# Four modulation blocks of layer 0 moved behind the first feed-forward units, and layer 1's column sums taken two units later, in a two-block fp32 kernel

## The chip, the cores and the metric

The kernel runs on one core of one Trainium2 chip. The metric is the device time of one execution in microseconds (us); the median of the runs shown is quoted. The tensor engine (TensorE, PE in the profile) multiplies, the vector engine (VectorE, DVE) and the scalar engine (ScalarE, ACT) evacuate and prepare operands, GpSimd (POOL) helps, and SyncE (SP) issues nearly all weight transfers from one in-order queue.

## The reference, cut to what matters

The program computes two blocks on a latent sequence of 512 rows and a context of 256 rows, width 1024, all in fp32. Only the first block matters here. It has two layers, a Fourier mixer layer (i = 0) and a differential attention layer (i = 1), and each begins with its modulation vectors:

```
for i in range(DEPTH):
    sh1, sc1, g1, sh2, sc2, g2 = split(silu(c)     @ w_ada[i] + b_ada[i], 6)
    csh1, csc1, cg1, csh2, ...  = split(silu(c_ctx) @ w_ada[i] + b_ada[i], 6)
    x = x + g1 * mixer(modulate(rms_norm(x), sh1, sc1))
    x = x + g2 * swiglu(modulate(rms_norm(x), sh2, sc2), ffn_w_in[i], ffn_w_out[i])
    (the same for ctx, in layer 0)
```

So each layer has a matrix w_ada[i] of 1024 x 6144 (24 MB) that is multiplied with only two vectors (the latent's condition and the context's). The kernel cuts it into 24 blocks of 256 columns, 1 MB each. Blocks 0 to 3 give sh1, 4 to 7 sc1, 8 to 11 g1, 12 to 15 sh2, 16 to 19 sc2 and 20 to 23 g2. The last four of layer 0, which give g2, are used only when a product of the first feed-forward is added to x.

## The kernel before, in words

**One stream of weights.** `stream_plan` writes down every weight block in the order in which it is loaded, and SP issues the loads in that order. The first 24 loads (`EARLY`) rotate over six buffers (two of `ring` and four of `early`, which are later overwritten by the split weights); all later ones alternate over the two buffers of `ring`. Before SP issues a load it waits until the block before it in the same buffer has been used (`blocks_used`), and everything behind it in the queue waits too.

**The front.** The order is: 24 modulation blocks of layer 0, four blocks of the Fourier layer's output weights (`fnet`, each from two sources, 4 transfers), then the feed-forward. In the front TensorE runs the DFT of x, and in between takes each modulation block as strips: `ada_rows` multiplies its eight 128-row pieces with the two conditions in four 32-column strips of the array (L677), VectorE copies the result to SBUF, `ada_cols` turns and sums it into columns (L688), and VectorE adds the bias. Blocks 16 to 19 of the order come beside the last DFT feature products; then comes `dft_middle` (L785), then blocks 20 to 23 in a loop of their own, then `x_turned` (L758, L760) for four pieces of x, the meta rows (L827), and the first `fnet` product (L845). The first `fnet` block is prepared by GpSimd (a sum and a difference of its halves, L2965 and L2967), split by ScalarE (`split_hi`, which waits until all 24 front blocks have been used) and VectorE (`split_lo`).

**Split weights.** Every weight block of 128x2048 is split into a high and a low part (ScalarE L1682, VectorE L2359) into one of two buffers, two units ahead of TensorE: in the slot after unit c the block of unit c+2 is split. TensorE makes three products for each piece of 128 rows (high by high, high by low, low by high).

**The first feed-forward.** A layer's feed-forward has 22 "in" units and three groups of four "down" units: in 0 to 7, down 0 to 3 of group 0, in 8 to 15, down 0 to 3 of group 8, in 16 to 21, down 0 to 3 of group 16 (with 6 pieces instead of 8). A unit is 96 matmuls (L649 with 512 columns, L654 with 256). After an in unit ScalarE and VectorE gate it (L2464, L2467), ScalarE rounds `hid`, VectorE makes its low part (L2471), and the split follows; after a down unit VectorE adds to x (`residual`, L2445).

**Layer 1's modulation beside it.** Its 24 blocks are streamed between the units: block k comes directly behind the weights of unit k+1. Blocks 0 to 21 are summed by VectorE at the end of the slot of in unit k (`sum_ada`: 16 instructions of 128x256, L2272 and L2275), and TensorE takes the column sums at the end of in unit k+1 (`ada_reduce`, eight small matmul records, L698), waiting for VectorE's `ada_acc`. Blocks 22 and 23 are taken as strips on TensorE (`strips` L709 and `strip_cols` L716) beside the down units of the last group. There is no modulation block beside the other down units.

Of the kernel before, what the change touches and what calls it, by code (L numbers as in the profile page):

```python
# [12 lines left out]
P = 128  # L13
D = 1024
KC = D // P
# [14 lines left out]
EARLY = 24  # L30
# [58 lines left out]
ADA0 = [4, 5, 6, 7, 0, 1, 2, 3] + list(range(8, 24))  # L89
# [42 lines left out]
def stream_plan():  # L132
# [3 lines left out]
    for layer in range(2):  # L136
        late = []
        for lo, hi in GROUPS:
            units = [("in", layer, c) for c in range(lo, hi)] + [("down", layer, lo, cb) for cb in range(4)]
            for unit in units:  # L140
                plan += [unit] + late
                late = []
                if layer == 0 and unit[0] == "in":
                    late = [("ada", 1, unit[2])]
                elif (layer, hi) == (0, FC) and unit[3] < 2:
                    late = [("ada", 1, FC + unit[3])]
        if layer == 0:
            plan += DIFF
# [16 lines left out]
def bass_two_blocks_kernel(nc, io, kt_d, dl_d, dc_d, xsave, out):  # L165
# [36 lines left out]
    with ExitStack() as ctx:  # L202
# [234 lines left out]
        def blocks_used(key):  # L437

            if key[0] == "ada":
                if key[1] and key[2] < FC:  # L440
                    return ada_acc, key[2] + 1
                return ada_row, 25 + key[2] - FC if key[1] else AT0[key[2]] + 1
            if key in NARROW:
                return q_lo, 4 * Q_OF[key] + 4
            return w_lo, W_OF[key] + 1
# [174 lines left out]
        def _(pe):  # L620
# [70 lines left out]
            def ada_reduce(b):  # L691

                pe.wait_ge(ada_acc, b + 1)
                pe.wait_ge(ada_taken, 24 + b - 1)
                for j in range(2):
                    for c in range(2):
                        o = 4 * j + 2 * c
                        m = nc.tensor.matmul(bank[6 + b % 2][:, o:o + 2], adacc[:, b % 2, c, P * j:P * j + P], ones[:, 0:2],  # L698
# [3 lines left out]
            def strips(b):  # L702

                n = N_OF[("ada", 1, b)]
                pe.wait_ge(ring_ready[slot_of(n)], arrived(n))
                pe.wait_ge(ada_taken, 24 + b - 1)
                for kc in range(KC):
                    q = 32 * (kc % 4)
                    m = nc.tensor.matmul(bank[6 + b % 2][q:q + 32, 0:256], condz[:, kc, :], slot(n)[:, kc, :], start=kc < 4, stop=kc >= 4)  # L709
                m.then_inc(ada_row, 1)  # L710

            def strip_cols(b):

                pe.wait_ge(ada_ev, 24 + b - FC + 1)
                for j in range(2):
                    m = nc.tensor.matmul(bank[6 + b % 2][:, 256 + 2 * j:258 + 2 * j], adacc[:, b % 2, 0, P * j:P * j + P], sel,  # L716
                                         start=True, stop=True)
                m.then_inc(ada_done, 1)

            def norm_sums(i, with_ctx):  # L720
# [3 lines left out]
                if i == 1:  # L724
                    pe.wait_ge(ada_taken, 24)
# [93 lines left out]
            for i in range(20, 24):  # L819
                ada_rows(i)  # L820
                ada_cols(i - 1)
            ada_cols(23)
# [1403 lines left out]
        def _(dve):  # L2226
# [17 lines left out]
            def take_ada(layer, b):  # L2244

                dve.wait_ge(ada_done, 24 * layer + (b if layer else AT0[b]) + 1)
                o, o2 = 48 * layer + 2 * b, 2 if layer and b < FC else 1
                c = 256 if layer and b >= FC else 0
                src = bank[6 + b % 2][:, c:c + 4 * o2].rearrange("p (a n k) -> p a n k", a=2, k=o2)[:, :, :, 0]
# [3 lines left out]
            def ada_out(i):  # L2253
# [5 lines left out]
                if i:  # L2259
                    take_ada(0, ADA0[i - 1])  # L2260

            def sum_ada(b):

                n = N_OF[("ada", 1, b)]
                dve.wait_ge(ring_ready[slot_of(n)], arrived(n))
                dve.wait_ge(ada_done, 24 + b - 1)
# [108 lines left out]
            take_ada(0, ADA0[7])  # L2375
# [15 lines left out]
            for i in range(20, 24):  # L2391
                ada_out(i)
            take_ada(0, 23)
# [62 lines left out]
            def ffn(layer):  # L2456
                end = ROWS if layer == 0 else LAT
                for g, (lo, hi) in enumerate(GROUPS):
                    for k in range(lo, hi):
# [14 lines left out]
                        if layer == 0:  # L2474
                            if k:
                                take_ada(1, k - 1)
                            sum_ada(k)
                    for cb in range(4):
                        residual(T_OF[("down", layer, lo, cb)], layer, 5, cb, layer == 0)
                        split_lo(S_OF[("down", layer, lo, cb)] + NS)  # L2480
                        if (layer, hi) == (0, FC) and cb < 3:
                            take_ada(1, FC - 1 + cb)
                            if cb < 2:
                                dve.wait_ge(ada_row, 25 + cb)
                                nc.vector.tensor_copy(adacc[:, cb, 0, :], bank[6 + cb][:, 0:256]).then_inc(ada_ev, 1)
# [686 lines left out]
```

## Time and profile before

| | |
|---|---|
| median of 3 runs | 2629.66 us (2626.38 to 2633.78) |
| the profiled execution's own time | 2629.45 us |
| its span, first to last instruction | 2627.7 us |
| TensorE busy | 2443.8 us, 93% of the span |
| VectorE, ScalarE, GpSimd busy | 1274.8, 904.7, 379.5 us |
| mean granted TensorE clock | 0.963 |
| the front up to the first `fnet` product | 124.2 us |
| the first feed-forward, from in unit 1 to the last down unit | 193.3 to 777.4 us |

Times in the trace count from the first instruction. The busy time of TensorE says how full it is, not whether it is fast: a matmul at half clock is busy for longer. So the waits of TensorE and its granted clock are read together.

### The profile page before, as it was taken

The numbers are of one execution on the slowest core, as the hardware profiler recorded it, in microseconds if no ns is written. First come the engines' busy times: TensorE is split into PE (matmuls) and PEld (weight loads), VectorE is DVE, ScalarE is ACT, GpSimd is POOL, SyncE is SP. The second block draws the span as 40 slices with busy tenths as digits, with TensorE's granted clock in tenths as the row PEclk, the third lists the DMA queues.
The fourth block names the chain that finished last, engine by engine and source line by source line (L and its number), as shares of the span: only waits on it lengthen the run. The fifth ranks groups of instructions, "written<-read, shape, count | busy, mean of one in ns | idle before, by whom it ended". The sixth has DMA issues, their size and how long they took to land.

```text
span 2627.7 us, 34491 instructions
## 1 busy us (share of the span) xinstructions
PE 2443.8 (93%) x14270; PEld 2041.1 (78%) x14270; DVE 1274.8 (49%) x2067; ACT 904.7 (34%) x1480; POOL 379.5 (14%) x311
## 2 busy tenths in 40 slices
PE   7799999999989999979999989898989989999998
PEld 3588788888868777657888869787878768777777
DVE  1585534544546777764333354455554344444433
ACT  2241111111223544433222234454545233444421
POOL 0230000000015534310000010322334210000000
PEclk9899999999999999989999989899999989999998
DMA  9823332332431111012333331121211121111222
GB/s 319 238 81 96 106 103 81 113 112 65 121 120 33 42 39 49 33 48 80 97 96 96 88 120 49 33 65 65 65 49 65 49 65 50 55 59 49 80 96 89
DMA packets 252064, 220.71 MB, mean 84 GB/s; under 512 B 7352, under 2 KB 243283, under 8 KB 251524
## 3 DMA queue, kind: packets, MB, share of 16 engines
q1 hardware_dynamic: 248392, 217.86, 26.8%
q8 instruction: 113, 1.85, 0.3%
q10 hardware_dynamic: 3260, 0.58, 0.1%
q14 instruction: 43, 0.35, 0.0%
q0 software_dynamic: 256, 0.07, 0.0%
HBM read 214.23 MB, written 6.26 MB: 84 GB/s over the span
## 4 chain that ended last, share of the span: by engine, by line
PE 54%; ACT 5%; DVE 5%; issue 3%; POOL 2%; DMA 0%; DVEq 0%; POOLq 0%; ACTq 0%
PE two L649 10%; PE bank L1430 4%; PE bank L649 3%; PE bank L1246 3%; PE bank L1250 3%; PE bank L1230 3%; PE two L1192 3%; PE bank L1411 2%; PE bank L979 2%; PE bank L1113 2%; PE two L1450 2%; PE two L1087 1%; PE two L1207 1%; PE bank L949 1%; PE bank L961 1%
## 5 line engine op out<-in xcount | busy, mean ns | idle before, releaser
L2370 DVE TENSOR_TENSOR wL<-ring,wH 128x512 fp32r<-128x512 f32 x224 | 171.2, 778 | 264.4 <-ACT wH L1691 264.2
L2359 DVE TENSOR_TENSOR wL<-ring,wH 128x2048 fp32r<-128x2048 f32 (+1 forms) x80 | 179.0, 2237 | 229.3 <-ACT wH L1682 229.0
L1682 ACT ACTIVATE wH<-ring 128x2048 fp32r<-128x2048 f32 (+1 forms) x80 | 149.4, 1868 | 351.2 <-DMA ring<-in_ffn_w_out 75.1
L649 PE MATMUL two<-h1H,wH 128*128 128x512 f32 x496 | 197.2, 398 | 0.0
L649 PE MATMUL two<-h1L,wH 128*128 128x512 f32 x496 | 194.9, 393 | 0.0
L649 PE MATMUL two<-h1H,wL 128*128 128x512 f32 x496 | 194.8, 393 | 0.0
L1691 ACT ACTIVATE wH<-ring 128x512 fp32r<-128x512 f32 x224 | 134.0, 624 | 69.0 <-PE bank L1230 29.2
L2275 DVE SCALAR_TENSOR_TENSOR adacc<-ring,cond,adacc 128x256 f32<-128x256 f32 x308 | 123.8, 478 | 0.0
L2974 POOL TENSOR_TENSOR rstd<-rstd,sq 128x768 f32<-128x768 f32 (+1 forms) x15 | 30.7, 2044 | 612.5 <-ACT sq L1718 611.4
L1250 PE MATMUL bank<-unH,wH 128*128 128x272 f32 (+1 forms) x384 | 117.9, 307 | 0.0
L1753 ACT ACTIVATE gateS<-two 128x512 f32<-128x512 f32 x44 | 26.3, 598 | 262.6 <-PE bank L654 105.0
L1250 PE MATMUL bank<-unH,wL 128*128 128x272 f32 (+1 forms) x384 | 111.1, 289 | 0.0
L1250 PE MATMUL bank<-unL,wH 128*128 128x272 f32 (+1 forms) x384 | 111.1, 289 | 0.0
L649 PEld LDWEIGHTS two<-h1H,wL 128*128 128x128 f32 x496 | 94.2, 190 | 20.3
L649 PEld LDWEIGHTS two<-h1H,wH 128*128 128x128 f32 x496 | 94.5, 191 | 18.8
L649 PEld LDWEIGHTS two<-h1L,wH 128*128 128x128 f32 x496 | 94.5, 190 | 18.8
L2445 DVE SCALAR_TENSOR_TENSOR xT<-two,ada,xT 128x512 f32<-128x512 f32 (+1 forms) x48 | 30.6, 679 | 153.3 <-PE bank L654 51.7
L649 PE MATMUL two<-hidH,wH 128*128 128x512 f32 x264 | 104.1, 394 | 0.0
L649 PE MATMUL two<-hidL,wH 128*128 128x512 f32 x264 | 103.4, 392 | 0.0
L649 PE MATMUL two<-hidH,wL 128*128 128x512 f32 x264 | 103.2, 391 | 0.0
L2137 ACT ACTIVATE probA<-two,amx 128x144 f32<-128x144 f32 (+3 forms) x64 | 34.7, 541 | 154.7 <-DVE amx L2842 154.6
L1430 PE MATMUL bank<-unH,wH 128*128 128x512 f32 x192 | 83.6, 436 | 0.5 <-ACT vA L2110 0.5
(600 smaller groups left out, 6994.7 us busy)
## 6 DMA issues: line engine op xcount, KB each, us to landing
ring<-in_ffn_w_in SPq DMA_DIRECT2D x88, 512.0 KB
ring<-in_w_in SPq DMA_DIRECT2D x40, 1024.0 KB
ring<-in_w_ada SPq DMA_DIRECT2D x32, 1024.0 KB
early<-in_w_ada SPq DMA_DIRECT2D x16, 1024.0 KB, 11.3
ring<-in_ffn_w_out SPq DMA_DIRECT2D x16, 1024.0 KB
ring<-in_diff_w_in SPq DMA_DIRECT2D x12, 1024.0 KB
ring<-in_w_proj_ssd SPq DMA_DIRECT2D x8, 1024.0 KB
ring<-in_ffn_w_out SPq DMA_DIRECT2D x8, 768.0 KB
```

The costliest lines, as they stand in the source:

```text
L649: m = nc.tensor.matmul(bank[3 * s + half], w, r[:, 0:LAT], start=i == 0, stop=i == n - 1)
L979: m = nc.tensor.matmul(bank[b][:, 256 * (i % 2):256 * (i % 2) + 256], h2[x][:, kc, i * P:(i + 1) * P], w[y][:, kc, :], start=k == 0, stop= ...
L1192: m = nc.tensor.matmul(o[:, at:at + hi - lo], w[y][:, kc, P * j:P * j + P], a[x][:, kc, lo:hi], start=k == 0, stop=k == 3 * KC - 1)
L1230: m = nc.tensor.matmul(bank[b], w[y][:, kc, P * t:P * t + P], ys[x][:, kc, :], start=k == 0, stop=k == 11)
L1246: m = nc.tensor.matmul(bank[b][:, 256 * (t % 2):256 * (t % 2) + 256], un[x][:, kc, META + P * t:META + P * t + P], w[y][:, kc, :], start=k ...
L1250: m = nc.tensor.matmul(bank[b][:, 0:hi - lo], w[y][:, kc, P * j:P * j + P], un[x][:, kc, lo:hi], start=k == 0, stop=k == 3 * KC - 1)
L1430: m = nc.tensor.matmul(bank[6 + j], w[y][:, kc, P * j:P * j + P], un[x][:, kc, META:ALL], start=k == 0, stop=k == 3 * KC - 1)
L1682: nc.scalar.activation(hi, raw, ACT.Copy).then_inc(w_hi, 1)
L1691: nc.scalar.activation(hi[:, 2 * r:2 * r + 2, :], raw[:, 2 * r:2 * r + 2, :], ACT.Copy, scale=colA[:, c:c + 1] if SPLIT[n][0] == "ps" else ...
L2275: m = nc.vector.scalar_tensor_tensor(out=o, in0=w[:, kc, :], scalar=x, in1=o, op0=ALU.mult, op1=ALU.add)
L2359: nc.vector.tensor_tensor(lo, raw, hi.bitcast(F32), ALU.subtract).then_inc(w_lo, 1)
L2370: nc.vector.tensor_tensor(lo, raw, hi.bitcast(F32), ALU.subtract).then_inc(q_lo, 1)
```

## The change

Layer 0's last four modulation blocks (20 to 23) leave the front: `EARLY` is 20, the stream goes from the 20th modulation block directly to `fnet`, and ScalarE's first split waits for 20 blocks. A list `MORE` has the 28 blocks that are left (layer 0's four, then layer 1's 24), and `MORE_AT` gives each unit of the first feed-forward its block: every in unit and the first three down units of each group, in order, until the 28 are placed (in units 0 to 7 take blocks 0 to 7 of the list, down units 0 to 2 of group 0 take 8 to 10, in 8 to 15 take 11 to 18, down 0 to 2 of group 8 take 19 to 21, in 16 to 21 take 22 to 27). Each is streamed directly behind the weights of the next unit. The first four, layer 0's, are taken as strips by TensorE at the end of in units 0 to 3. All 24 of layer 1 are now summed by VectorE (two more than before), and TensorE takes the column sums of a block at the end of the second unit after the block's own (`sum_cols(j - 2)`), not of the first. VectorE waits for layer 0's 24th block before the first residual.

```diff
-EARLY = 24
+EARLY = 20
-ADA0 = [4, 5, 6, 7, 0, 1, 2, 3] + list(range(8, 24))
+ADA0 = [4, 5, 6, 7, 0, 1, 2, 3] + list(range(8, EARLY))
+MORE = [("ada", 0, b) for b in range(EARLY, 24)] + [("ada", 1, b) for b in range(24)]
+NSTRIP = 24 - EARLY
+MORE_AT = {key: j for j, key in enumerate(sum([[("in", 0, c) for c in range(lo, hi)] + [("down", 0, lo, cb) for cb in range(3)]
+                                              for lo, hi in GROUPS], []))}
...
             for unit in units:
                 plan += [unit] + late
-                late = []
-                if layer == 0 and unit[0] == "in":
-                    late = [("ada", 1, unit[2])]
-                elif (layer, hi) == (0, FC) and unit[3] < 2:
-                    late = [("ada", 1, FC + unit[3])]
+                j = MORE_AT.get(unit, len(MORE))
+                late = MORE[j:j + 1]
...
+            def more_columns(key):
+
+                j = MORE_AT.get(key)
+                if j is None:
+                    return
+                if 1 <= j <= NSTRIP:
+                    strip_cols(j - 1)
+                if j < NSTRIP:
+                    strips(j)
+                if NSTRIP <= j - 2 < len(MORE):
+                    sum_cols(j - 2)
...
             dft_middle()
-            for i in range(20, 24):
-                ada_rows(i)
-                ada_cols(i - 1)
-            ada_cols(23)
+            ada_cols(EARLY - 1)
...
-                        if layer == 0:
-                            ada_reduce(c - 1)
+                        more_columns(("in", layer, c))
...
-                        if (layer, hi) == (0, FC):
-                            if cb == 0:
-                                ada_reduce(FC - 1)
-                            if cb in (1, 2):
-                                strip_cols(FC + cb - 1)
-                            if cb < 2:
-                                strips(FC + cb)
+                        more_columns(("down", layer, lo, cb))
...
+            def more_sums(key):
+
+                j = MORE_AT.get(key)
+                if j is None:
+                    return
+                if j < NSTRIP:
+                    strip_out(j)
+                if 1 <= j <= NSTRIP:
+                    take_ada(EARLY + j - 1)
+                if NSTRIP <= j - 2 < len(MORE):
+                    take_ada(EARLY + j - 2)
+                if NSTRIP <= j < len(MORE):
+                    sum_ada(j)
...
-            for i in range(20, 24):
-                ada_out(i)
-            take_ada(0, 23)
+            take_ada(EARLY - 1)
...
                         split_lo(S_OF[("in", layer, k)] + NS)
-                        if layer == 0:
-                            if k:
-                                take_ada(1, k - 1)
-                            sum_ada(k)
+                        more_sums(("in", layer, k))
                     for cb in range(4):
+                        if (layer, g, cb) == (0, 0, 0):
+                            dve.wait_ge(ada_taken, 24)
                         residual(T_OF[("down", layer, lo, cb)], layer, 5, cb, layer == 0)
                         split_lo(S_OF[("down", layer, lo, cb)] + NS)
-                        if (layer, hi) == (0, FC) and cb < 3:
-                            take_ada(1, FC - 1 + cb)
...
+                        more_sums(("down", layer, lo, cb))
```

`sum_cols` and `ada_reduce` issue the same matmuls; `strips` and `strip_cols` are the functions of before with another index.

## Rows read from the trace of the kernel before

**Rows 1.** The page's line of engines: busy us, share of the span, instructions.
```profile
PE 2443.8 (93%) x14270; PEld 2041.1 (78%) x14270; DVE 1274.8 (49%) x2067; ACT 904.7 (34%) x1480; POOL 379.5 (14%) x311
```
**Rows 2.** TensorE's waits from 96 to 173 us: total, times, longest.
```profile
PE bank L677 <- DMA early<-in_w_ada: 4.3, 2, 4.2
```
**Rows 3.** TensorE's waits from 193.3 to 777.4 us, the first feed-forward.
```profile
PE bank L698 <- DVE adacc L2275: 12.0, 7, 3.1
PE bank L709 <- DMA ring<-in_w_ada: 3.4, 1, 3.4
```
**Rows 4.** Windows: length, TensorE busy (matmuls), granted clock, DMA share, GB/s.
```profile
104.00:124.00 20.00, 10.18 (x56) 0.51 0.41 93
...
285.00:292.00 7.00, 6.14 (x19) 0.51 0.75 226
...
482.00:490.00 8.00, 7.25 (x22) 0.57 0.85 240
...
728.00:739.00 11.00, 6.55 (x31) 0.54 0.65 205
```
**Rows 5.** Timeline of SyncE, 92 to 108 us: start, duration, what.
```profile
95.18 2.86 SPq L573 DMA_DIRECT2D ring<-in_fnet_w_out  x1
```
**Rows 6.** Timeline of all engines, 108 to 125 us; idle before in brackets.
```profile
112.06 2.82 POOL L2965 TENSOR_TENSOR wsum<-ring 128x1024 f32<-128x1024 f32 x1 [15.67 <-DMA ring<-wback]
...
112.53 2.38 DVE L2403 TENSOR_SCALAR ng<-ada 128x16 f32<-128x16 f32 x1
...
118.31 1.03 PE L827 MATMUL bank<-kt,mraw 16*128 16x16 f32 x8
...
124.06 0.60 SPq L573 DMA_DIRECT2D ring<-in_fnet_w_out  x1
...
124.18 0.66 PE L845 MATMUL two<-uvH,wH 128*128 128x386 f32 x1 [4.83 <-DVE wL L2357]
```
**Rows 7.** Windows of 1 us (length, granted clock, DMA share, GB/s) behind that issue.
```profile
131.00:132.00 1.00, 1.00 0.15 46
```
**Rows 8.** Timeline of TensorE at 96, 210, 228 and 750 us.
```profile
96.36 1.51 PE L785 MATMUL two<-RS,kt 128*32 128x257 f32 x32
...
209.96 0.95 PE L698 MATMUL bank<-kt,adacc 128*128 128x2 f32 x8
...
227.56 0.95 PE L698 MATMUL bank<-kt,adacc 128*128 128x2 f32 x8
...
750.16 0.50 PE L716 MATMUL bank<-kt,adacc 128*128 128x2 f32 x4
...
751.59 0.50 PE L649 MATMUL two<-hidH,wH 128*128 128x512 f32 x1
```
**Rows 9.** Timeline of VectorE, 193 to 213 us: the slot of in unit 0.
```profile
194.48 0.69 DVE L2464 TENSOR_TENSOR gateS<-gateS,two 128x512 f32<-128x512 f32 x1 [4.95 <-ACT gateS L1756]
...
196.41 0.96 DVE L2471 TENSOR_TENSOR hidL<-gateS,hidH 128x768 fp32r<-128x768 f32 x1 [0.91 <-ACT hidH L1760]
198.22 2.29 DVE L2359 TENSOR_TENSOR wL<-ring,wH 128x2048 fp32r<-128x2048 f32 x1 [0.85 <-ACT wH L1682]
...
200.95 5.63 DVE L2275 SCALAR_TENSOR_TENSOR adacc<-ring,cond,adacc 128x256 f32<-128x256 f32 x14
211.14 0.69 DVE L2464 TENSOR_TENSOR gateS<-gateS,bank 128x512 f32<-128x512 f32 x1 [4.56 <-ACT gateS L1756]
```
**Rows 10.** Timeline of SyncE, 420 to 545 us: loads of modulation blocks.
```profile
422.97 0.37 SPq L591 DMA_DIRECT2D ring<-in_w_ada  x1
...
521.13 0.37 SPq L591 DMA_DIRECT2D ring<-in_w_ada  x1
...
539.83 0.37 SPq L591 DMA_DIRECT2D ring<-in_w_ada  x1
```
**Rows 11.** Timeline of VectorE, 376 to 396 us: two down units without blocks.
```profile
376.44 2.19 DVE L2445 SCALAR_TENSOR_TENSOR xT<-two,ada,xT 128x512 f32<-128x512 f32 x4 [12.29 <-PE two L654]
...
393.12 0.75 DVE L2445 SCALAR_TENSOR_TENSOR xT<-two,ada,xT 128x512 f32<-128x512 f32 x1 [12.29 <-PE bank L654]
```

More of the change, by code:

```diff
@@ L437, in blocks_used @@
         def blocks_used(key):
+            if key in MORE:
+                j = MORE.index(key)
+                return (ada_row, EARLY + j + 1) if j < NSTRIP else (ada_acc, j - NSTRIP + 1)
             if key[0] == "ada":
-                if key[1] and key[2] < FC:
-                    return ada_acc, key[2] + 1
-                return ada_row, 25 + key[2] - FC if key[1] else AT0[key[2]] + 1
+                return ada_row, AT0[key[2]] + 1
             if key in NARROW:
@@ L689, in ada_cols, with strips @@
                 m.then_inc(ada_done, 1)
[L691 to L695, printed above, removed]
+            def strips(j):
+                n = N_OF[MORE[j]]
+                pe.wait_ge(ring_ready[slot_of(n)], arrived(n))
+                pe.wait_ge(ada_taken, EARLY + j - 1)
+                for kc in range(KC):
+                    q = 32 * (kc % 4)
+                    m = nc.tensor.matmul(bank[6 + j % 2][q:q + 32, 0:256], condz[:, kc, :], slot(n)[:, kc, :], start=kc < 4, stop=kc >= 4)
+                m.then_inc(ada_row, 1)
@@ new lines, in strip_cols, with sum_cols @@
+            def strip_cols(j):
+                pe.wait_ge(ada_ev, EARLY + j + 1)
+                for h in range(2):
+                    m = nc.tensor.matmul(bank[6 + j % 2][:, 256 + 2 * h:258 + 2 * h], adacc[:, j % 2, 0, P * h:P * h + P], sel,
+                                         start=True, stop=True)
+                m.then_inc(ada_done, 1)
+            def sum_cols(j):
+                pe.wait_ge(ada_acc, j - NSTRIP + 1)
+                pe.wait_ge(ada_taken, EARLY + j - 1)
+                for h in range(2):
@@ L696, in ada_reduce @@
                     for c in range(2):
-                        o = 4 * j + 2 * c
-                        m = nc.tensor.matmul(bank[6 + b % 2][:, o:o + 2], adacc[:, b % 2, c, P * j:P * j + P], ones[:, 0:2],
+                        o = 4 * h + 2 * c
+                        m = nc.tensor.matmul(bank[6 + j % 2][:, o:o + 2], adacc[:, j % 2, c, P * h:P * h + P], ones[:, 0:2],
                                              start=True, stop=True)
                 m.then_inc(ada_done, 1)
[L702 to L718, printed above, removed]
+            def more_columns(key):
[8 more added lines that the diff above has]
+                    sum_cols(j - 2)
@@ L724, in norm_sums @@
                 if i == 1:
-                    pe.wait_ge(ada_taken, 24)
+                    pe.wait_ge(ada_taken, EARLY)
                 for k, x in enumerate((part, sq[:, 0], sq[:, 1])):
@@ L2242, in _, with take_ada @@
             nc.vector.tensor_copy(negR[:], negm).then_inc(s_round, 1)
[L2244 to L2249, printed above, removed]
+            def take_ada(i):
+                dve.wait_ge(ada_done, i + 1)
+                _, layer, b = (("ada", 0, ADA0[i]) if i < EARLY else MORE[i - EARLY])
+                o, k, c = 48 * layer + 2 * b, 2 if i >= 24 else 1, 256 if EARLY <= i < 24 else 0
+                src = bank[6 + i % 2][:, c:c + 4 * k].rearrange("p (a n k) -> p a n k", a=2, k=k)[:, :, :, 0]
                 nc.vector.tensor_tensor(ada[layer][:, 2 * b:2 * b + 2, :], src,
@@ L2374, in _ @@
                 ada_out(i)
-            take_ada(0, ADA0[7])
+            take_ada(7)
             multipliers(0)
```

14 lines of the change are left out of this document (8 added, 6 removed).

## The prediction, made before the changed kernel was run

> **What bounds the kernel now.** I read the page first. TensorE is busy 93% of the span [rows 1], so its waits are few and each is worth finding; the other engines have room on average. Then I listed TensorE's waits in the two stretches that the change touches. In the front it waits 4.3 us for the modulation blocks, almost all of it for block 23, and 4.8 us for the first `fnet` weights [rows 2, 6]. In the first feed-forward it waits 12.0 us in seven places for VectorE's sums and 3.4 us for one strip block [rows 3]. Third, the windows with the granted clock: it is at the lower of its two levels (0.5, 1.2 GHz) from about 104 to 128 us after TensorE had idled, and again after three of the waits in the feed-forward [rows 4]. Last, the timelines of SyncE, VectorE and TensorE, to see who is late for whom.
>
> **The front.** Removed: four loads of 1 MB, four times strips and columns on TensorE, four copies and additions on VectorE. Today `dft_middle` starts at 96.36 [rows 8] and ends at 97.9; the four blocks and the wait for the last fill the time to 110.3, then come `x_turned` and the meta rows, which end at 118.31 + 1.03 = 119.34, and the first `fnet` product starts 4.84 us later, behind ScalarE's and VectorE's split [rows 6]. After the change the chain is: ada_cols of block 19 to about 98.3; `x_turned` 4 at 99.3 (it needs the last feature copy); its third piece needs VectorE, which after 99.3 has some 2 us of small work and one copy, so about 102.3; meta rows done at 105.7 (the same instructions with the clock still up for most of them); plus 4.84: 110.6. The other chain into the same start is the load. Its first issue is at 95.18 [rows 5], behind strips 18 and not behind the four blocks, so it hardly moves; today its data come through a queue that still holds 4 MB and GpSimd starts on them at 112.06 [rows 6], while the third `fnet` block, alone in the queue, is issued at 124.06 [rows 6] and its traffic ends in the microsecond after 131 [rows 7], some 7.4 us later. So the first lands near 102.5, GpSimd needs 2.8 + 2.4 us, ScalarE and VectorE 2.3 us behind that, and this chain ends near 110. The two meet; I take 110.6, a gain of 124.2 - 110.6 = 13.6 us. What follows (four `fnet` blocks, norm, modulation) hangs on this start and moves with it. Bounds: 9 us if the `fnet` load is no faster than today relative to its neighbours, 15.5 if the clock stays up.
>
> There is a collision in this stretch. VectorE's `ng`, sixteen columns, took 2.38 us and ended when GpSimd's sum that began 0.47 us earlier ended [rows 6]. The Trainium skill, SBUF — State Buffer, Who interferes with whom, says that the two share a port pair and that the second to issue is blocked until the first finishes; the trace agrees. By that rule the same 2.4 us can fall on a copy of `x_turned` in the new order, which is inside the lower bound above.
>
> **Work on TensorE in the feed-forward.** A down unit without a block repeats after 393.12 - 376.44 = 16.68 us [rows 11], an in unit with column sums after 227.56 - 209.96 = 17.60 us [rows 8], so column sums cost 0.92 us. Strips with the columns of the block before cost 751.59 - 750.16 = 1.43 us [rows 8]. Added: four strips and two more column sums; removed: two strips. That is 2 x 1.43 + 2 x 0.92 = 4.7 us, and it lies on the bounding engine, nothing covers it. The Trainium skill, TensorEngine Tiling, Key Properties, says that changing the tiling mode drains the engine, which speaks against moving strips between dense matmuls; the row from the end of one tile to the start of the next holds both changes of mode and is 1.43 us, so no more than this is charged.
>
> **Waits removed there.** 12.0 + 3.4 = 15.4 us [rows 3]. At half clock TensorE loses half of the slow time in which it is busy: 3.0, 3.1 and 3.1 us in the three windows [rows 4], 9.2 in all. Together 24.6; less the added 4.7 the feed-forward would be 19.9 us shorter if no new wait came.
>
> **Where the stall goes.** SyncE issues a modulation block when VectorE has finished the one before, and the next unit's weights behind it; these must land, be split by ScalarE and VectorE, and only then VectorE sums the next block. This loop is a chain. Its length is the distance of the issues: (521.13 - 422.97)/5 = 19.6 us with in weights, 539.83 - 521.13 = 18.7 with down weights [rows 10]; of twenty such issues three stand there. It is longer than TensorE's 17.6, so each block in a row makes VectorE 2.0 us (or 1.1) later relative to TensorE. Today the sums are due after one unit and the delay shows as the seven waits. Measured from the end of the unit on TensorE (1.18 us before the gate starts, 211.14 against 209.96 [rows 8, 9]), the first sum ends 200.95 + 5.63 - (194.48 - 1.18) = 13.3 us after it. With sums due a unit later they are never late. Next late are the split weights of unit c+2: they are done 206.58 - 200.51 = 6.1 us before the sum ends [rows 9] and due 17.6 + 0.9 us after the unit's end, so the sum's end may slip to 24.6. And at the change from in to down units the last `hid` low part is due about 5.7 us after the unit's end and takes 2.9 us from the start of the gate [rows 9], which starts only when VectorE has finished the previous sum.
>
> Group by group. In units 0 to 3 have strips, which release their buffer at once, so the loop starts at in 4 with 13.3. Six loops follow before the free slot (one in, four down, one in weight): 13.3 + 2 x 2.0 + 4 x 1.1 = 21.7, under 24.6, no wait. Behind the slot of down 3, which has no block, the backlog drains, but two loads and splits of about 10 us each still run in series, so in 8 starts at about 14.5. Five in loops give 24.5, the sixth (down weights) 25.6: VectorE is 8.0 us into the next slot, its low part comes at 8.0 + 2.9 = 10.9 instead of 5.7, and TensorE waits 5.2 us. Four more loops bring 26.1 at down 2, where 24.6 - 0.9 is allowed: 2.4 us. The last group has six in units and short down weights and stays under the limit. New waits 7.6 us, and one of them longer than the longest of today, 3.1 us [rows 3], which a slow window follows, so I charge one more slow stretch, 3.1 us. So 10.7 of the 19.9 us come back as waits for other tiles, and 9.2 stay.
>
> **The sum.** Against the profiled execution, 2629.45 us (span 2627.7, 1.75 around it, 0.2 under the median of the runs): 2629.45 - 13.6 - 9.2 = 2607 us. VectorE's two additional sums cost nothing by themselves: the work of a slot is about 13 us and the loop is charged already. The moved 4 MB cost no transfer time of their own: even in the crowded windows behind a stall the DMA share is 0.65 to 0.85 [rows 4].
>
> **The rivals.**
> - *No new waits.* The loop shortens, since SyncE's data come sooner when TensorE doesn't stall: at 19.0 and 18.2 us group 8 ends under its limits. For it: the last group ran at 19.2. Against it: group 0 ran at 20.0. 2629.45 - 13.6 - 19.9 = 2596 us.
> - *The loop takes all of it back.* There are 16 loops in the two long groups and (24.6 - 13.3) + (24.6 - 14.5) = 21.4 us of slack, so with a mean excess x over TensorE's unit the waits are 16x - 21.4. They reach 19.9 at x = 2.6, a mean loop of 20.2 us (two of five loops in group 8 were as long). Only the front is left: 2616 us.
> - *The front gives less.* The two halves of a `fnet` load write half of the partitions each, and the stretch in which they ran moved only 93 GB/s [rows 4]; if the first load is the bound, GpSimd starts at 107 and the front gains 6 us: 2614 us.
> - *Slower.* The same loop at more than 17.6 + (33.5 + 21.4)/16 = 21.0 us in the mean gives waits above 33.5 us, which is all that front and feed-forward together can save (13.6 + 19.9), and each group then stays late through the down units too, where there were no blocks before. At 21.5 with three slow stretches it is 16 x 3.9 - 21.4 + 10 = 51 us of waits, 2629.45 - 33.5 + 51 = 2647 us. For it: two loops in group 0 took 20.9 and 20.7. Against it: these were loops in which TensorE itself stalled, and every loop with down weights was under 19.5.
>
> **How the numbers follow.** Forecast 0.50, no new waits 0.17, all taken back 0.16, less front 0.10, slower 0.04, and 0.03 for a result near no change, by a mix that I don't see. The forecast's own range is 2600 to 2614 (front 13.6 with 2 either way, new waits and clock 10.7 with 5 either way). To leave out no more than 2 in 10 the range reaches from the case without waits to the one in which all is taken back: 2595 to 2617. About 0.3%, 8 us, is what a measurement here can tell from no change, so faster means under 2621.8: the first four cases, 0.93; same 0.03; slower 0.04.
>
> **What would show each step.** The first `fnet` product at 110 to 111; a DMA queue that is empty when its load is issued. No wait of TensorE for `adacc` at the column sums. Waits of TensorE for `hidL` at the first down unit of group 8 and for `wL` around its end, 5 to 9 us together, none in group 0. The distance of SyncE's modulation loads at 19 to 20 us in in units. From in unit 1 to the last down unit 575 us instead of 584. The prediction is wrong if the first `fnet` start moves by less than 9 us, or if TensorE waits for weights in more than about six places.

## The result, and the profile after

The changed kernel takes 2614.37 us (median of 5 runs, 2609.34 to 2616.35), against 2629.66 before: ratio 0.994 with a 95% interval of 0.9923 to 0.9957. It is faster by 0.6%, which is 15 us. The forecast was 2607 us with a range of 2595 to 2617: the sign is right and the time lies in the range, but the gain was put half as high again as it is.

The page of the changed kernel: the span, and the line of engines that answers to [rows 1].

```profile
span 2607.6 us, 34472 instructions
...
PE 2425.3 (93%) x14246; PEld 2027.8 (78%) x14246; DVE 1283.9 (49%) x2097; ACT 904.9 (35%) x1480; POOL 378.7 (15%) x311
```

The profiled executions differ by 20.1 us (2629.45 and 2609.34), more than the medians, which differ by 15.3. So I cut each profile into three parts: up to the first `fnet` product (front), from there to the end of the first feed-forward, and the rest, which the change doesn't touch. The first rows are of the pair, the others of the experiments below.

| kernel | first `fnet` product | in unit 1 starts | feed-forward ends | in unit 1 to end | TensorE's waits in it | rest after it |
|---|---|---|---|---|---|---|
| before | 124.18 | 193.30 | 777.20 | 583.9 | 15.4 | 1850.5 |
| changed | 113.32 | 183.85 | 761.93 | 578.1 | 11.1 | 1845.6 |
| changed, again | 112.80 | 183.03 | 761.22 | 578.2 | 12.5 | 1844.6 |
| one-unit lag | 113.03 | 183.54 | 771.03 | 587.5 | 11.6 | 1852.9 |
| sums alone | 120.15 | 188.87 | 765.11 | 576.2 | 14.2 | 1850.5 |
| order | 113.50 | 184.41 | 745.34 | 560.9 | 0 | 1851.9 |
| gap | 113.39 | 184.24 | 756.48 | 572.2 | 6.9 | 1844.0 |
| buffers | 114.87 | 185.13 | 765.24 | 580.1 | 11.8 | 1846.7 |
| order, one-unit lag | 114.16 | 185.14 | 746.06 | 560.9 | 0 | 1852.4 |
| order, `fnet` ahead | 114.44 | 183.82 | 744.74 | 560.9 | 0 | 1847.0 |

The first two parts became 777.20 - 761.93 = 15.3 us shorter, just the difference of the medians. The other 4.9 us of the pair lie in the rest, where all ten profiles have the same work and spread over 1844 to 1853 us. That spread is the clock's: the rest with the shortest time (gap) has a granted clock of 0.97 and keeps TensorE busy for 1708.1 us, the longest (one-unit lag) has 0.96 and 1718.3 us, with the same 9929 matmul records. Had I read the profiled pair alone, I would have credited the change with them.

**The front** gained 124.18 - 113.32 = 10.9 us, forecast 13.6. The timeline of all engines, 103 to 114 us, answers to [rows 6]; before it the row of SyncE that answers to [rows 5].

```profile
94.44 0.70 SPq L575 DMA_DIRECT2D ring<-in_fnet_w_out  x1
```
```profile
103.47 0.67 PE L838 MATMUL bank<-kt,mraw 16*128 16x16 f32 x8
...
104.94 2.33 POOL L2983 TENSOR_TENSOR wsum<-ring 128x1024 f32<-128x1024 f32 x1 [8.58 <-DMA ring<-wback]
107.35 2.35 POOL L2985 TENSOR_TENSOR ring<-ring 128x1024 f32<-128x1024 f32 x1
...
109.73 1.06 ACT L1684 ACTIVATE wH<-ring 128x1024 fp32r<-128x1024 f32 x1 [1.31 <-POOL ring L2985]
...
111.96 1.22 DVE L2382 TENSOR_TENSOR wL<-ring,wH 128x1024 fp32r<-128x1024 f32 x1
...
113.32 0.66 PE L856 MATMUL two<-uvH,wH 128*128 128x386 f32 x1 [9.18 <-DVE wL L2382]
```

TensorE's own chain was faster than forecast: the meta rows end at 103.47 + 0.67 = 104.14, not 105.7, and then it is idle for 9.18 us. It waits for VectorE's low part, that for ScalarE, that for GpSimd, and GpSimd for the load. The load was issued 0.74 us earlier than before and landed at 104.94, which is 10.5 us after its issue. Windows of the same stretch (length; busy time and count of TensorE's matmuls, its weight loads, VectorE, ScalarE and GpSimd; then granted clock, DMA share and GB/s) show that the DMA engines had nearly nothing to do when it was issued:

```profile
90.00:94.00 4.00, 4.00 (x55) 2.59 (x55) 1.71 (x6) 0.98 (x2) 0.00 (x0) 1.00 0.06 20
94.00:96.00 2.00, 2.00 (x30) 1.16 (x22) 1.05 (x4) 0.00 (x0) 1.53 (x2) 1.00 0.06 11
```

VectorE's `ng`, which took 2.38 us in [rows 6], took 0.17 us here, at 101.20, with GpSimd idle. The Trainium skill, SBUF — State Buffer, Who interferes with whom, says that only the shared port pair causes contention; the trace agrees, since `ng` was quick where GpSimd didn't run. It didn't matter for the time, since VectorE wasn't on the chain that ended last. The same block on a copy of `x_turned`, which I had feared, doesn't show even in the trace of before: two such copies from 114.83 on took 1.28 us together beside a GpSimd operation of 114.96 to 117.32, and two took 1.28 us here, at 101.28, with GpSimd idle.

**The first feed-forward.** TensorE's waits from in unit 1 to the end, in answer to [rows 3] (total, times, longest):

```profile
PE two L651 <- DVE wL L2384: 6.2, 4, 2.4
PE two L651 <- DVE hidL L2494: 3.8, 1, 3.8
PE two L651 <- issue: 1.0, 1, 1.0
```

No wait for `adacc` and none for a strip block is left. In their place stand the two kinds that were forecast, for `wL` and `hidL`. The longest is at the first down unit of group 8; an unforecast one is in group 8 itself, before in 14 (timeline of TensorE at the two places):

```profile
486.05 0.47 PE L651 MATMUL two<-h1H,wH 128*128 128x512 f32 x1 [2.22 <-DVE wL L2384]
...
533.07 0.50 PE L651 MATMUL two<-hidH,wH 128*128 128x512 f32 x1 [3.84 <-DVE hidL L2494]
```

VectorE's timeline has the same moment from the other side. It finishes the sum of in 14's block, starts the gate of in 15 at once with no idle time before it, and so ends the low part of `hid` only at 533.02, when TensorE has waited 3.84 us for it:

```profile
524.60 5.62 DVE L2300 SCALAR_TENSOR_TENSOR adacc<-ring,cond,adacc 128x256 f32<-128x256 f32 x14
530.14 0.68 DVE L2487 TENSOR_TENSOR gateS<-gateS,bank 128x512 f32<-128x512 f32 x1
...
532.06 0.96 DVE L2494 TENSOR_TENSOR hidL<-gateS,hidH 128x768 fp32r<-128x768 f32 x1 [0.91 <-ACT hidH L1765]
```

SyncE's timeline gives the loop, in answer to [rows 10]: (511.47 - 410.13)/5 = 20.3 us from one modulation load to the next in group 8, where a TensorE unit has 17.6.

```profile
410.13 0.37 SPq L593 DMA_DIRECT2D ring<-in_w_ada  x1
...
430.74 0.37 SPq L593 DMA_DIRECT2D ring<-in_w_ada  x1
...
511.47 0.37 SPq L593 DMA_DIRECT2D ring<-in_w_ada  x1
```

Three of the waits are followed by a stretch at the lower clock, as in [rows 4] (same columns as the windows above):

```profile
486.00:490.00 4.00, 3.95 (x11) 3.12 (x12) 4.00 (x12) 0.00 (x0) 0.00 (x0) 0.59 0.00 0
534.00:538.00 4.00, 4.00 (x24) 4.00 (x22) 0.00 (x0) 0.00 (x0) 0.00 (x0) 0.57 0.99 321
602.00:606.00 4.00, 3.24 (x8) 2.60 (x9) 4.00 (x12) 0.00 (x0) 0.00 (x0) 0.59 0.00 0
```

From its first product to its column sums a unit takes 16.78 us at the full clock (430.91 to 447.69). The three with these stretches took 18.39, 22.40 (3.84 of it the wait) and 18.38 us, so the clock cost 1.6 + 1.8 + 1.6 = 5.0 us.

### The profile page after: what moved, and what is told of

Read it like the earlier page. It is cut to its first block, busy times and chain, and to the rows that moved or that the text cites. A ratio compares the mean times of both kernels' runs of the same rounds, so it can differ in the third digit from the quotient of the medians.

```text
span 2607.6 us, 34472 instructions
## 1 busy us (share of the span) xinstructions
PE 2425.3 (93%) x14246; PEld 2027.8 (78%) x14246; DVE 1283.9 (49%) x2097; ACT 904.9 (35%) x1480; POOL 378.7 (15%) x311
## 4 chain that ended last, share of the span: by engine, by line
PE 54%; DVE 5%; ACT 5%; issue 3%; POOL 2%; DMA 0%; DVEq 0%; POOLq 0%; ACTq 0%
PE two L651 10%; PE bank L1435 4%; PE bank L651 3%; PE bank L1251 3%; PE bank L1255 3%; PE bank L1235 3%; PE two L1197 3%; PE bank L1416 2%; PE bank L984 2%; PE bank L1118 2%; PE two L1455 2%; PE two L1092 1%; PE two L1212 1%; PE bank L954 1%; PE bank L966 1%
## 5 line engine op out<-in xcount | busy, mean ns | idle before, releaser
L2300 DVE SCALAR_TENSOR_TENSOR adacc<-ring,cond,adacc 128x256 f32<-128x256 f32 x336 | 135.0, 477 | 0.0
L651 PEld LDWEIGHTS two<-h1H,wL 128*128 128x128 f32 x496 | 94.0, 189 | 20.3
L1765 ACT ACTIVATE hidH<-gateS 128x768 fp32r<-128x768 f32 (+1 forms) x44 | 32.5, 739 | 169.4 <-DVE gateS L2487 117.7
## 6 DMA issues: line engine op xcount, KB each, us to landing
early<-in_w_ada SPq DMA_DIRECT2D x12, 1024.0 KB, 11.8
```

What stands on the lines that cost most here:

```text
L651: m = nc.tensor.matmul(bank[3 * s + half], w, r[:, 0:LAT], start=i == 0, stop=i == n - 1)
L2300: m = nc.vector.scalar_tensor_tensor(out=o, in0=w[:, kc, :], scalar=x, in1=o, op0=ALU.mult, op1=ALU.add)
```

## The experiments

All ratios stand against runs of the kernel before, made beside them on the same chip; "under" and "over the changed kernel" is against its 2614.37 us, where nothing else is said. In the expectations, L is the loop theory of the prediction.

**One-unit lag.** Everything as changed, but a block's column sums are due after one unit again.

```diff
-                if NSTRIP <= j - 2 < len(MORE):
-                    sum_cols(j - 2)
+                if NSTRIP <= j - 1 < len(MORE):
+                    sum_cols(j - 1)
```
(the same in `more_sums`, for `take_ada`)

> The changed kernel, with layer 1's column sums taken one unit behind their block again, everything else left. Theory L (a loop of loads, splits and sums is longer than TensorE's unit and the later due time only adds slack): with the due time at the next unit's end only 17.6 us after the unit are allowed for the sum instead of 24.6, so the seven to thirteen places where the sum is later than that show as waits for adacc in every group; I expect 16 to 22 us of waits in the first feed-forward instead of 11, with one to three more slow stretches of the clock, and 2614 + 8 to 12 = 2622 to 2626 us. Theory F (only the front counts, the two units change nothing): 2614 us.

Measured: 2625.36 us, ratio 0.9974 (0.9963 to 0.9985), 11 us over the changed kernel. TensorE's waits in the feed-forward:

```profile
PE bank L718 <- DVE adacc L2300: 11.6, 7, 2.8
```

So the later due time is worth about 10 us: the shorter front with sums due after one unit leaves 0.3% only. Theory L had the total right and one of its two parts wrong. It said that the waits would grow to 16 or more; they are hardly longer in sum than with the two-unit lag (11.1). What grew is the slow stretches, five instead of three, as L allowed, but three of the five are twice as long (windows; the last three of each row are clock, DMA share, GB/s):

```profile
345.00:350.00 5.00, 4.61 (x17) 3.84 (x18) 2.44 (x5) 0.00 (x0) 0.00 (x0) 0.66 0.69 220
455.00:460.00 5.00, 5.00 (x17) 3.95 (x17) 0.96 (x1) 0.85 (x1) 0.00 (x0) 0.66 1.06 308
492.00:500.00 8.00, 7.23 (x22) 5.97 (x23) 2.60 (x5) 1.00 (x2) 0.00 (x0) 0.58 0.83 237
551.00:558.00 7.00, 6.68 (x20) 5.62 (x21) 2.37 (x5) 0.00 (x0) 0.00 (x0) 0.52 0.84 265
728.00:736.00 8.00, 6.28 (x20) 5.33 (x21) 3.77 (x9) 1.34 (x1) 0.00 (x0) 0.57 0.63 195
```

That is 27 us at the lower clock against 10, worth some 8 us: nearly all of 587.5 - 578.1 = 9.4. The rival theory F is refuted, since the lag does matter.

**Sums alone.** The front as before, with the change's sums for layer 1 and their two-unit lag.

```diff
-EARLY = 20
+EARLY = 24
...
             dft_middle()
+            for i in range(20, EARLY):
+                ada_rows(i)
+                ada_cols(i - 1)
             ada_cols(EARLY - 1)
```
(and `ada_out` for the same four on VectorE)

> The second part of the change alone: all 24 blocks of layer 0 stay in the front as before, layer 1's 24 blocks are all summed by VectorE beside in and the first three down units, columns two units behind. Theory L: the front is that of before (first fnet product at 124); the feed-forward loses the strips but now has two runs of eleven blocks in a row, so VectorE gets late in group 0 as well: 14 to 18 us of waits for wL and hidL, 4 to 7 us of clock; 2622 to 2627 us. Theory S (the two parts are independent and this one alone brings what is left after the front's 11): 2625 us with waits as in the changed kernel, 11 us, all behind in 8.

Measured: 2617.71 us, 0.9959 (0.9947 to 0.9971). The waits are of the same kinds as in the changed kernel. The large `hidL` waits lie at the first down units of groups 0 and 8 (2.3 us between 300 and 345 us, beside the 1.5 us put down to issue, and 3.5 us behind 500; the third is of 0.5 us at 718), as L has it: no unit has strips here, so the loop runs from in 0 on, and group 0 has waits too.

```profile
PE two L651 <- DVE wL L2387: 6.4, 4, 3.1
PE two L651 <- DVE hidL L2499: 6.3, 3, 3.5
PE two L651 <- issue: 1.5, 1, 1.5
```

So L's waits are right (14.2 us, it gave 14 to 18), and S, with 11 us and all of it behind in 8, is refuted. The time is better than either theory gave. The table shows where: the front, which has the work of before, is 4 us shorter than there. Two windows of this kernel show why (the last three of a row: clock, DMA share, GB/s):

```profile
80.00:84.00 4.00, 4.00 (x34) 1.90 (x26) 0.96 (x4) 0.00 (x0) 0.00 (x0) 0.50 1.07 336
...
104.00:124.00 20.00, 12.95 (x93) 10.96 (x93) 8.75 (x21) 4.96 (x9) 10.39 (x6) 0.71 0.60 122
```

TensorE was at the lower clock early, from 78 us on, while the DMA engines were full. It came later to block 23, waited 0.55 us for it instead of 4.2 [rows 2], and then lost the full clock only in the first half of `x_turned` (four of its products take 1.06 us at 109.70 and 0.60 at 112.79), where [rows 4] has 0.51 for the whole stretch. The parts add up within the noise: 0.41% for the sums alone and 0.26% for the front with a one-unit lag, 0.60% for both. But 4 us of the sums alone lie in a front with the work of before, so by stage the agreement is in part luck.

**Order.** If SyncE's queue closes the loop, then a modulation block that stands one place further back must break it: the weights of the next units no longer stand behind an issue that waits for VectorE's last sum. Blocks, sums and the two buffers are the same; only `stream_plan` differs.

```diff
-                late = MORE[j:j + 1]
+                late, soon = soon, MORE[j:j + 1]
```
(with both empty at the start)

> The changed kernel with one edit in the plan: each modulation block is streamed behind the weights of the second next unit, not of the next, so that the weights no longer stand behind a load that waits for VectorE's sum. Same work, same slots of the sums. Theory L (the loop through SyncE's queue makes VectorE late): the loop is cut, the sum ends about 13 to 15 us after each unit throughout, TensorE has no waits for wL or hidL in the first feed-forward, it takes 562 to 564 us instead of 578; 2598 to 2600 us. Theory D (VectorE is late because its own work, or DMA bandwidth, in a slot is too much): waits stay near 11 us, 2612 to 2615 us.

Measured: 2598.36 us, 0.9877 (0.9864 to 0.989), 16 us under the changed kernel. TensorE has no wait in the whole feed-forward, and is at the full clock in all of it (one window):

```profile
184.40:745.30 560.90, 560.90 (x3332) 497.17 (x3329) 292.60 (x562) 100.99 (x106) 11.65 (x5) 1.00 0.37 113
```

SyncE issues the modulation blocks every 17.6 us now, in step with TensorE, and the weights go out by themselves between them:

```profile
425.30 0.37 SPq L593 DMA_DIRECT2D ring<-in_w_ada  x1
436.75 0.99 SPq L589 DMA_DIRECT2D ring<-in_ffn_w_in  x2
442.89 0.37 SPq L593 DMA_DIRECT2D ring<-in_w_ada  x1
```

The idle time of VectorE shows the loop most directly. In the changed kernel it has no idle time before the gates from 450 to 530 us, the later part of group 8, but in the middle of each of these slots it stands idle for 7.6 to 9.7 us, waiting for the high part of weights that came late. First a row of the changed kernel, then the same operation here:

```profile
483.61 2.29 DVE L2384 TENSOR_TENSOR wL<-ring,wH 128x2048 fp32r<-128x2048 f32 x1 [9.69 <-ACT wH L1687]
```
```profile
469.61 2.29 DVE L2384 TENSOR_TENSOR wL<-ring,wH 128x2048 fp32r<-128x2048 f32 x1 [0.84 <-ACT wH L1687]
```

Here VectorE finishes each sum and is then idle for 5.4 us before the next gate:

```profile
490.01 5.63 DVE L2300 SCALAR_TENSOR_TENSOR adacc<-ring,cond,adacc 128x256 f32<-128x256 f32 x14
501.06 0.69 DVE L2487 TENSOR_TENSOR gateS<-gateS,two 128x512 f32<-128x512 f32 x1 [5.42 <-ACT gateS L1761]
```

This settles the mechanism. The same sums by the same engine from the same number of buffers cost TensorE nothing once the queue doesn't chain them to the weights; neither VectorE's work nor transfer time was the limit, which refutes D. It also checks my price of the work: 583.9 less the 24.6 of waits and clock, plus one strip (1.43) net and two column sums (1.84) from in 1 on, is 562.6, measured 560.9, so it is right within 1.7 us.

**Gap.** The loop is interrupted once: unit in 12 has no block, and the later blocks move up by a place.

```diff
-MORE_AT = {...sum([[("in", 0, c) for c in range(lo, hi)] + ...
+MORE_AT = {...sum([[("in", 0, c) for c in range(lo, hi) if c != 12] + ...
```

> The changed kernel with one edit in the map of blocks to units: in 12 takes no block, so the run of eleven sums in a row in group 8 becomes four and seven, and the last block is summed beside the first down unit of the last group. Same sums, same stream rule. Theory L (the loop makes VectorE later by some 2.5 us for each block in a row, and a slot without a block lets it catch up): the waits of 10 us in and behind group 8 vanish, at most 2 us of waits stay, and with them the three slow stretches go; the first feed-forward takes 563 to 565 us instead of 578, 2600 to 2602 us. Theory D (VectorE's or the DMA engines' load in a slot is itself too much): about the same waits elsewhere, 2612 to 2615 us.

Measured: 2604.37 us, 0.9902 (0.9887 to 0.9918), 8 us under the changed kernel run beside it (2612.47). The waits before in 14 and at group 8's first down unit are gone, as L says (the backlog must build up first). This alone doesn't refute D, since a slot that is too full would build up a backlog too; the order experiment does. And L was too hopeful: the feed-forward took 572.2 us, not 563 to 565, with two slow stretches left, and 6.9 us of waits are left where L left 2 at most, at 378, 572, 591, 728 and 744 us:

```profile
PE two L651 <- DVE wL L2384: 6.9, 5, 2.6
```

Those at 572 and 591 us (0.63 and 2.35) stand before the last down unit of group 8 and before in 16, as in the changed kernel (0.77 and 2.35): behind the gap SyncE's issues are 19.8 to 20.3 us apart with down weights too, so six blocks in a row fill the slack again. The one at 728 us (2.59) is new; it stands in the last group, which now has seven blocks in a row where it had six.

**Order, with the one-unit lag.** Both edits from above together.

> The load order of the run before (each modulation block behind the weights of the second next unit) together with column sums one unit behind their block, not two. Theory L: with the loop cut the sum ends about 14 to 16 us after its unit, before the 17.6 us of the next unit's end, so the later due time is worth nothing any more: no wait for adacc, 2598 to 2600 us. Theory T (two units are needed in any order): waits for adacc as with the old order, 10 us and some slow stretches, 2607 to 2614 us.

Measured: 2600.26 us, 0.9886 (0.9872 to 0.9901), no different from the order alone, again 560.9 us without a wait. So the two-unit lag is worth 10 us where the loop drags and nothing where it doesn't.

**Changed kernel, again**, beside the second set of experiments.

> The changed kernel itself once more, beside the next three on one chip. Every theory: 2614 us, give or take 3; ratio 0.994.

Measured: 2612.47 us, 0.9938 (0.9917 to 0.9958). The stages of its profile agree with the first within 1 us (table). The parts inside the feed-forward vary more: 12.5 us of waits, one of them of 3.15 us for `hidL` at 712 us, in the last group, where the first profile has none, but two slow stretches instead of three. Waits and clock together are 12.5 + 3.4 = 15.9 us here and 16.1 in the first profile.

**Buffers.** For the front: the last two modulation blocks of the front (18 and 19 of the order) go to two of the `early` buffers and not to the two of `ring`, so that the first `fnet` block follows block 12 in its buffer, which comes free earlier than behind block 18.

```diff
-            return n % (NR + 4) if n < EARLY else (n - EARLY) % NR
+            if n < EARLY - NR:
+                return n % (NR + 4)
+            return NR + n - (EARLY - NR) if n < EARLY else (n - EARLY) % NR
```

> The changed kernel with the last two front blocks loaded into two of the early buffers instead of the two ring buffers, so that the first fnet loads wait for the blocks 12 and 13 of the order, used at 81 and 82 us, not for 18 and 19 (94.3, 95.8). Theory N (after the change the first fnet product is bound by the landing of its load, issued at 94.4 and landed at 104.9, with the DMA engines idle from 90 to 95): the load is issued at 87 or 88, GpSimd starts by 98, and the product is bound by the turned x and the meta rows instead, which end at 104.1, plus 4.8: 109 instead of 113.3, so 4 us less: 2610 us. Theory O (the start is bound on TensorE's or ScalarE's side anyway): no change, 2614 us.

Measured: 2616.59 us (2607.49 to 2625.14), 0.9953 (0.9935 to 0.997): no gain. Blocks 18 and 19 now had to wait for the use of blocks 14 and 15, and the `fnet` loads, behind them in the queue, were issued at 91.06, not at 87 or 88. The transfers fell together, TensorE waited 1.41 us for a modulation block, and GpSimd started on `fnet` at 106.42, later than in the changed kernel:

```profile
99.97 1.07 PE L681 MATMUL bank<-early,condz 128*32 128x256 f32 x16 [1.41 <-DMA early<-in_w_ada]
```

In this profile TensorE also ran 10.2 us at the lower clock from 78 us on, so as a test of the load's place it is inconclusive.

**Order, `fnet` ahead.** The same question built better, on the kernel with the new order: the first `fnet` block is streamed before the last two front blocks.

```diff
+AHEAD = EARLY - 2
+FRONT = [n % 6 for n in range(AHEAD)] + [0, 2, 3, 1]
...
-    plan += [("fnet", cb) for cb in range(4)]
+    plan.insert(AHEAD, ("fnet", 0))
+    plan += [("fnet", cb) for cb in range(1, 4)]
...
-            return n % (NR + 4) if n < EARLY else (n - EARLY) % NR
+            return FRONT[n] if n < len(FRONT) else (n - len(FRONT)) % NR
...
```

> The load order of the run before, and the first fnet block loaded ahead of the last two front blocks, which go to early buffers. Theory N (landing of the first fnet block at 105 us binds the first fnet product): it is issued at 81 us while the DMA engines are busy anyway, GpSimd starts before 98, and the product is bound by the meta rows plus 4.8 us; these slip by up to 2 us, as the last two blocks land later. First fnet product at 109 to 111 instead of 113.5, 2595 us. Theory O (TensorE waits for the delayed last two blocks by as much as is won): no difference, 2598 us.

Measured: 2604.05 us (2593.55 to 2607.71), 0.9899 (0.988 to 0.9917), not better than the order alone. The load did come early: GpSimd starts at 93.10, 12 us sooner. The start of `fnet` then hangs on TensorE's own chain, the meta rows, which end at 108.95 + 0.67 = 109.62, and the 4.83 us behind them that [rows 6] had:

```profile
93.10 2.42 POOL L2986 TENSOR_TENSOR wsum<-ring 128x1024 f32<-128x1024 f32 x1 [10.10 <-DMA ring<-wback]
```
```profile
108.95 0.67 PE L841 MATMUL bank<-kt,mraw 16*128 16x16 f32 x8
...
114.44 0.66 PE L859 MATMUL two<-uvH,wH 128*128 128x386 f32 x1 [4.83 <-DVE wL L2385]
```

The meta rows end 5.5 us later than in the changed kernel, for two reasons in the trace: 1.39 us of wait for one of the delayed blocks, and 10.2 us at the lower clock from 78.8 us. By the starts of the feature product (77.51, against 78.22 in the changed kernel) the second cost 5.5 + 0.7 - 1.4 = 4.8 us, about half its length, so without it `fnet` would start near 110 by my estimate; no run here shows it.

By the medians the best version is thus the order alone, 2598.36 us: 1.2% under the kernel before and 0.6% under the changed one. Its interval overlaps with those of the two other kernels that have the new order.

## Why the prediction was right, and where its sizes were off

**Right:** the sign, the mechanism of the new waits, their tiles (`hidL` at the first down unit of group 8, `wL` around its end; the single waits were of other sizes, 3.84 us where I had 5.2, and none at down 2 where I had 2.4), that no `adacc` wait is left, and that the loop through SyncE's queue makes them. The order experiment shows that this loop is the cause, by removing it alone. The price of the added TensorE work was right as well: in 1, with columns and strips, takes 202.11 - 183.85 = 18.26 us, 1.58 more than the 16.68 of [rows 11], and 1.43 was charged. The rule of the Trainium skill, TensorEngine Tiling, Key Properties, that a change of mode drains the engine, adds nothing beyond that here.

**Front, 13.6 us, measured 10.9: 2.7 too much.** The main step that failed is "the first lands near 102.5". I took the 7.4 us of a `fnet` load that is alone in the queue, but the first has the second close behind it, four more transfers within 4 us, and took 10.5 us. In those 10 us (95 to 105) the DMA engines moved 1.50 MB, where the block that was alone needed 1.04 MB in all; so by the traffic it shared them with its successor, but no run leaves the successor out. A smaller step failed too: "ScalarE and VectorE 2.3 us behind that". GpSimd ended at 107.35 + 2.35 = 109.70 and the product started at 113.32, which is 3.6 us: ScalarE's second half takes 1.1 us, VectorE starts on the first only behind it, and needs 2.4 us for two. With GpSimd 0.4 us quicker that makes 2.4 + 1.3 - 0.4 = 3.3 us against the 110.0 of this chain. My two chains "meet" at 110; in fact TensorE's ended at 104.14 + 4.84 = 109.0, and the load's at 113.3. The sign that I had named, an empty queue at the issue, was there and proved nothing: the neighbour that shares the engines is issued after it, not before. That is the mechanism of "The front gives less" at half its size. `fnet` ahead showed the other side: with the load out of the way the start is 4.82 us behind the meta rows.

**New waits and clock, 10.7 us, measured 11.1 + 5.0 = 16.1: 5.4 too little.** The mechanism was right, the term of the sum mis-sized, in two ways. The loop in group 8 is 20.3 us long, where I took 19.6 from the mean of before: so the limit is reached one unit sooner, at in 14 (2.22 us), and small waits come for the weights of in 8 (0.87 us at 378) and in the down units of group 8 (0.77 us at 583). And three of the waits were followed by slow stretches, where I charged one, because I had tied them to a wait longer than 3.1 us; stretches of 3.4 us followed waits of 2.22, 2.35 and 3.84. "None in group 0" was wrong by the wait of 0.87 us at its end. There is a slip in the sum besides: from 25.6, four loops of 1.1 more and 5.2 less for the wait give 24.8 at down 2, not 26.1, so my own terms make 1.1 us of wait there and 6.3 in all, not 7.6.

Together: 24.6 - 4.7 - 16.1 = 3.8 us for the part from the first `fnet` product to the end of the feed-forward; measured (777.20 - 124.18) - (761.93 - 113.32) = 4.4, forecast 9.2. With the front it is 10.9 + 4.4 = 15.3 instead of 22.8 us, and the difference of 7.5 is the error of the forecast (2607 against 2614.4).

**The rivals.** "No new waits" (2596) isn't what this change does, but it is what the order experiment makes of it (2598). "All taken back" (2616) and "less front" (2614) each have nearly the right time for a wrong reason: the truth is a share of both, 5.4 and 2.7 us. The price of "less front" was wrong as well: a GpSimd start at 107 and my own 5.2 + 2.3 us behind it give 114.5, a gain of 9.7 and not 6, and so 2611 us. The formula of the two loop rivals, sixteen loops by their excess, fits: SyncE's issues in the changed kernel are 19.0 us apart in group 0 (five loops) and 19.9 in group 8 (nine, with the down weights), 19.6 in the mean, so 16 x 2.0 - 21.4 = 10.6 us, and 11.1 were measured. "All taken back" needed a mean of 20.2 and the slower case one of 21.0; the five loops with in weights of group 8 were 20.3 us in the mean, but the others pulled it down.

## What to carry to other kernels

In an in-order issue queue, look at what stands behind a load that waits for its buffer: a load that waits for a slow consumer chains that consumer to everything behind it, and moving it one place back was worth more here (16 us) than the whole change that was studied (15 us). More slack for a consumer that is late by a little each round only moves the wait to the next due thing; compare the length of the loop with the unit of the bounding engine first, and break it. A load's landing time is to be taken from a row in which its successors are issued as closely behind it as they will be, and each short wait of TensorE is to be charged with the slow stretch that may follow.

## What the runs showed of the hardware that I had not expected

The lower clock after a short idle time isn't decided by the length of that time. In the front TensorE idles 1.74 us for VectorE before the same feature product in all ten profiles. In six of them that product starts between 77.86 and 78.51 us, and TensorE goes on at the full clock. In four it starts between 77.22 and 77.51, and the clock falls behind it: for 10.2 us in sums alone, buffers and `fnet` ahead, and for 3.4 us in order with the one-unit lag. The rows ahead of the gap are the same instructions with the same durations; the whole front is merely some tenths of a microsecond earlier. First the changed kernel, then `fnet` ahead, TensorE's timeline:

```profile
78.22 1.52 PE L790 MATMUL two<-RS,kt 128*64 128x257 f32 x16 [1.74 <-DVE xT L2327]
79.67 1.07 PE L679 MATMUL bank<-ring,condz 128*32 128x256 f32 x16
```
```profile
77.51 1.59 PE L793 MATMUL two<-RS,kt 128*64 128x257 f32 x16 [1.74 <-DVE xT L2330]
...
79.04 1.94 PE L682 MATMUL bank<-ring,condz 128*32 128x256 f32 x16
```

The 16 strip matmuls behind it take 1.94 us instead of 1.07. What sets it wasn't tested. The Trainium skill, TensorE: Matmul & The Clock Gate, Part 1, says that the monitor behind the clock runs free and doesn't restart with a kernel. By that the same gap can go either way, which these profiles show, and the split by start time would be chance, which ten profiles can't tell. In `fnet` ahead the stretch cost 4.8 us of the front. It isn't what spreads that kernel's runs from 2593.55 to 2607.71 us: the profiled run, with the stretch in it, is the fastest of the five. The rest of the program, the same work in all ten profiles, spreads over 9 us, with the granted clock. Where differences of 5 us matter, a profiled pair can't give them; the medians with a table by stage can.

The loss can also go with a gain: in sums alone, slower early meant a wait of 0.55 us instead of 4.2, less time at the lower clock behind it, and a front that ended 4 us sooner.
